# FFN block couples: weight sums made by accumulating DMAs on GpSimd's queue instead of VectorE additions

## The reference, cut to what matters

```python
f = jnp.square(jax.nn.relu(rmsnorm(x, g_pre_ffn) @ w1)) @ w2
x = x + rmsnorm(f, g_post_ffn)
```

## Time and profile before

| | us |
|---|---|
| median of 3 runs | 1749.37 |
| the runs | 1748.9, 1749.37, 1751.52 |
| profiled execution, first to last instruction (span) | 1748.0 |
| TensorE busy | 1736.1 (99%) |
| VectorE busy | 1208.1 (69%) |
| ScalarE busy | 798.3 (46%) |
| GpSimd busy | 16.3 (1%) |
| share of the 16 DMA engines, data moved | 25.4%, 149.06 MB |

### The profile page before, as it was taken

How to read it: one execution, slowest core, us unless ns; L and a number is a source line. 1 busy time by engine, 2 the same in 40 slices (tenths; PEclk the granted TensorE clock), 3 DMA queues, 4 the chain that set the end, 5 groups by cost and what they waited for, 6 DMA issues and landing times.

```text
span 1748.0 us, 31686 instructions
## 1 busy us (share of the span) xinstructions
PE 1736.1 (99%) x12975; PEld 1722.7 (99%) x12975; DVE 1208.1 (69%) x2376; ACT 798.3 (46%) x1589; POOL 16.3 (1%) x23
## 2 busy tenths in 40 slices
PE   9999999999999999999999999999999999999998
PEld 8999999999999999999999999999999999999997
DVE  7665555658698787668687555556677897777665
ACT  7634333335465454436366343334345545444452
POOL 0100000000000000000000000000000000000000
PEclk9999999999999999999999999999999999999998
DMA  4321212232213222322122222121313213222221
GB/s 176 114 82 61 91 61 82 72 95 82 85 48 98 86 97 89 94 97 97 63 106 77 82 72 82 62 91 60 103 63 108 80 44 120 87 91 79 84 97 55
DMA packets 52032, 149.06 MB, mean 85 GB/s; under 512 B 5552, under 2 KB 17072, under 8 KB 51888
## 3 DMA queue, kind: packets, MB, share of 16 engines
q1 hardware_dynamic: 50608, 144.94, 25.4%
q10 hardware_dynamic: 1280, 2.10, 0.4%
HBM read 143.15 MB, written 3.87 MB: 84 GB/s over the span
## 4 chain that ended last, share of the span: by engine, by line
PE 98%; DVE 1%; DMA 1%; ACT 0%; SPq 0%; issue 0%; DVEq 0%
PE ring L708 20%; PE ring L710 20%; PE ring L709 20%; PE att L708 11%; PE att L710 11%; PE att L709 11%; PE att L2976 1%; PE att L703 1%; PE att L702 1%; PE att L715 0%; DMA w_raw<-blocks_in 0%; PE att L716 0%; DMA x<-x_in 0%; PE att L2791 0%; PE att L3032 0%; DVE last L2745 0%
## 5 line engine op out<-in xcount | busy, mean ns | idle before, releaser
L708 PE MATMUL ring<-xs_hi,w_lo 128*128 128x288 f32 x2272 | 675.1, 297 | 1.5 <-DVE xs_lo L1756 1.2
L710 PE MATMUL ring<-xs_hi,w_hi 128*128 128x288 f32 x2272 | 669.3, 295 | 0.0
L709 PE MATMUL ring<-xs_lo,w_hi 128*128 128x288 f32 x2272 | 669.0, 294 | 0.0
L708 PEld LDWEIGHTS ring<-xs_hi,w_lo 128*128 128x128 f32 x2272 | 426.6, 188 | 4.4 <-DVE w_lo L1742 1.1
L709 PEld LDWEIGHTS ring<-xs_lo,w_hi 128*128 128x128 f32 x2272 | 426.8, 188 | 1.6
L710 PEld LDWEIGHTS ring<-xs_hi,w_hi 128*128 128x128 f32 x2272 | 426.5, 188 | 0.0
L1742 DVE TENSOR_TENSOR w_lo<-w_raw,w_hi 128x1024 fp32r<-128x1024 f32 (+1 forms) x334 | 332.6, 1019 | 58.2 <-ACT w_hi L1213 47.7
L710 PE MATMUL att<-f_hi,w_hi 128*128 128x288 f32 x960 | 283.2, 295 | 0.0
L709 PE MATMUL att<-f_lo,w_hi 128*128 128x288 f32 x960 | 282.9, 295 | 0.0
L708 PE MATMUL att<-f_hi,w_lo 128*128 128x288 f32 x960 | 282.6, 294 | 0.0
L708 PEld LDWEIGHTS att<-f_hi,w_lo 128*128 128x128 f32 x960 | 180.4, 188 | 0.0
(11 more groups left out here) (292 smaller groups left out, 2601.5 us busy)
## 6 DMA issues: line engine op xcount, KB each, us to landing
w_raw<-blocks_in SPq DMA_DIRECT2D x235, 512.0 KB, 3.6
small_raw<-small_in SPq DMA_DIRECT2D x16, 320.0 KB, 3.9
small_raw<-small_in SPq DMA_DIRECT2D x32, 128.0 KB, 3.9
x<-x_in SPq DMA_DIRECT2D x8, 288.0 KB, 6.9
small_raw<-small_in SPq DMA_DIRECT2D x8, 192.0 KB, 4.3
kv_out<-kv ACTq DMA_DIRECT2D x2, 576.0 KB, 4.4
x_out<-x SPq DMA_DIRECT2D x1, 1152.0 KB, 5.3
small_raw<-small_in SPq DMA_DIRECT2D x2, 512.0 KB, 5.1
```

The lines of the kernel that those rows point to most:

```text
L708: pe.matmul(out, w[1], x[0], start=first, stop=False)
L709: pe.matmul(out, w[0], x[1], start=False, stop=False)
L710: return pe.matmul(out, w[0], x[0], start=False, stop=last)
```

## The change: what it does

The four sums of a couple are no longer made by VectorE. SyncE loads base values into the slots of the sums, straight from the weights in HBM, and GpSimd's queue issues four DMAs that add to them:

- left slot (s[2]): SyncE loads a11 into both halves (one DMA whose source repeats, 512 KB); GpSimd adds a21 to both halves (512 KB, `left_first`), giving a11 + a21 twice; then it adds a22 to half 0 (256 KB, `sum2_made`). Half 0 is then S2, half 1 is S3.
- right slot (s[3]): SyncE loads a21 into half 0, GpSimd adds a22 (256 KB, `sum1_made`): S1. SyncE loads a12 into half 1, GpSimd adds half 0 of the left slot to it (256 KB, from SBUF, `sum4_made`): S4.

Each step waits for the semaphore of the one it builds on. Since the sums now only add, S1, S2, S3 are other sums than before (S2 = a11 + a21 + a22, S3 = a11 + a21), and four of VectorE's steps on the products subtract where they added; the count and size of these stays. a21 is no longer loaded to the slot of the second block, of which SyncE loads 256 KB. High parts are copied 1024 wide for each of the two slots (2 instead of 4), low parts subtracted in 4 instructions a couple instead of 6; `left_lo` waits for `sum4_made`, since it overwrites the raw S2 that the fourth addition reads. TensorE's matmuls are the same in number and size; their waits are on the new counts.

The core of the diff (GpSimd's part, SyncE's part, VectorE's order; the same is done to the other places that called the removed functions):

```diff
+        def weight_sums(L, g, p):
+            s, at = slots_pair(g, p), based(L, g, p)
+            a21, a22 = (blocks[L * NB + n_w1(g, 2 * p + 1)][:, 512 * k:512 * (k + 1)] for k in range(2))
+            left, sum2 = pl.slot(s[2])[2], pl.half_slot(s[2], 0)[2]
+            sum1, sum4 = (pl.half_slot(s[3], k)[2] for k in range(2))
+            pool.wait_ge(pl.left_based, at)
+            pool.dma_start(left.rearrange("p (b k) -> p b k", b=2), a21.unsqueeze(1).broadcast_to([P, 2, 512]),
+                           accum_op=ALU.add).then_inc(pl.left_first, 16)
+            pool.wait_ge(pl.sum1_based, at)
+            pool.dma_start(sum1, a22, accum_op=ALU.add).then_inc(pl.sum1_made, 16)
+            pool.wait_ge(pl.left_first, at)
+            pool.dma_start(sum2, a22, accum_op=ALU.add).then_inc(pl.sum2_made, 16)
+            pool.wait_ge(pl.sum2_made, at)
+            pool.wait_ge(pl.sum4_based, at)
+            pool.dma_start(sum4, sum2, accum_op=ALU.add).then_inc(pl.sum4_made, 16)
...
+            def next_couple(g, p, g1, p1):
+                after_pair(g, p, 1)
+                pair_load(g1, p1, 0)
+                after_pair(g, p, 3)
+                left_base(g1, p1)
+                after_pair(g, p, 4)
+                pair_load(g1, p1, 1)
+                after_pair(g, p, 5)
+                sum1_base(g1, p1)
+                after_pair(g, p, 6)
+                sum4_base(g1, p1)
...
             after_w2(0, 0)
             pair_load(2, 0, 0)
+            left_base(2, 0)
             after_w2(0, 1)
             pair_load(2, 0, 1)
+            sum1_base(2, 0)
+            sum4_base(2, 0)
+            next_couple(2, 0, 2, 1)
             pair_load(3, 0, 0)
             pair_load(3, 0, 1)
+            after_w2(0, 3)
+            left_base(3, 0)
+            sum1_base(3, 0)
+            sum4_base(3, 0)
...
+                after_w2(g - 1, 2)
+                    left_base(g + 1, 1)
+                after_w2(g - 1, 3)
+                    sum1_base(g + 1, 1)
+                    sum4_base(g + 1, 1)
...
             def outs_and_lo(g, k0, g0, p0, g1, p1):
-                pair_sums(g1, p1)
                 f_done(g0, p0, 2)
                 w2_out(g, k0)
                 f_done(g0, p0, 3)
                 w2_out(g, k0 + 1)
-                lo_a22(g1, p1)
-                lo_s3(g1, p1)
+                block_lo(g1, p1)
                 w2_out(g, k0 + 2)
-                lo_a11(g1, p1)
-                lo_s12(g1, p1)
-                w2_out(g, k0 + 3)
-                lo_a12(g1, p1)
-                lo_s4(g1, p1)
-                for k in range(k0 + 4, k0 + 8):
+                half_lo(g1, p1)
+                for k in range(k0 + 3, k0 + 8):
                     w2_out(g, k)
+                left_lo(g1, p1)
+                right_lo(g1, p1)
...
             w2_out(0, 9)
-            lo_s3(2, 0)
-            lo_a11(2, 0)
-            lo_s12(2, 0)
+            half_lo(2, 0)
+            left_lo(2, 0)
             w2_out(0, 10)
-            lo_a12(2, 0)
-            lo_s4(2, 0)
+            right_lo(2, 0)
             mix_lo(pl.ml[0][:, :, :], pl.mraw[0][:, :, :], pl.mh[0][:, :, :], 18, 2)
...
             pair_c12(2, 1)
+            left_lo(3, 0)
+            right_lo(3, 0)
...
             pair_c12(7, 0)
+            left_lo(7, 1)
+            right_lo(7, 1)
...
-                s1, s2, s3, s4 = (pl.half_slot(s[i], k) for i in range(2, 4) for k in range(2))
+                s2, s3, s1, s4 = (pl.half_slot(s[i], k) for i in range(2, 4) for k in range(2))
...
-                eng.wait_ge(pl.pair_lo, n + 3)
+                eng.wait_ge(pl.pair_lo, n + 1)
                 product(0, a11, x_at(0, 0))
-                eng.wait_ge(pl.pair_lo, n + 5)
                 product(1, a12, x_at(4, 0))
                 eng.wait_ge(pl.mix_lo, 8 * L + 3)
+                eng.wait_ge(pl.pair_lo, n + 3)
                 product(2, s2, mixed(1))
...
                 product(4, a22, mixed(3))
+                eng.wait_ge(pl.pair_lo, n + 4)
                 product(5, s1, mixed(0))
```

More of the change, by code:

```diff
@@ L743, in program @@
         loads(nc, block, pl, x_in, consts, tables, blocks, small, uv, cache_t, cache_n, cache_pe, x_out)
-        key_rotation(nc, block, pl)
+        rotation_and_sums(nc, block, pl, blocks)
         scalar_engine(nc, block, pl, x_in, x_out, kv_out, kpe_out, conv_out)
@@ L960, in _ @@
             key_rope(L, 1)
+            for g in range(FIRST_PAIR, GROUPS):
+                for p in range(2):
+                    weight_sums(L, g, p)
         for i, (m0, m1) in enumerate(TAIL_MOVED):
@@ L1522, in half_hi, with left_hi, right_hi @@
                 act.activation(hi, raw, ACT.Copy).then_inc(pl.pair_hi, 1)
-            def sum_hi(g, p, made, i, k):
-                hi, _, raw = pl.half_slot(slots_pair(g, p)[i], k)
-                eng.wait_ge(pl.pair_sum, 4 * pair_no(L, g, p) + made)
+            def left_hi(g, p):
+                hi, _, raw = pl.slot(slots_pair(g, p)[2])
+                eng.wait_ge(pl.sum2_made, based(L, g, p))
                 act.activation(hi, raw, ACT.Copy).then_inc(pl.pair_hi, 1)
[L1529 to L1533, removed]
+            def right_hi(g, p):
+                hi, _, raw = pl.slot(slots_pair(g, p)[3])
+                eng.wait_ge(pl.sum1_made, based(L, g, p))
+                eng.wait_ge(pl.sum4_made, based(L, g, p))
+                act.activation(hi, raw, ACT.Copy).then_inc(pl.pair_hi, 1)
             normed_hi(0, 0, 4)
@@ L1544, in _ @@
             half_hi(2, 0)
-            sums_hi(2, 0)
+            left_hi(2, 0)
+            right_hi(2, 0)
             first_copy(2, 0)
@@ L1552, in _ @@
             half_hi(2, 1)
-            sums_hi(2, 1)
+            left_hi(2, 1)
+            right_hi(2, 1)
             block_hi(3, 0)
             half_hi(3, 0)
-            sum_hi(3, 0, 1, 2, 0)
             first_copy(2, 1)
-            sum_hi(3, 0, 2, 3, 0)
-            sum_hi(3, 0, 3, 2, 1)
-            sum_hi(3, 0, 4, 3, 1)
             pair_c11(2, 1)
             pair_c21(2, 1)
+            left_hi(3, 0)
             pair_c22(2, 1)
             pair_c12(2, 1)
+            right_hi(3, 0)
             first_copy(3, 0)
@@ L1586, in _ @@
                 half_hi(g, 1)
-                sums_hi(g, 1)
                 if g < GROUPS - 2:
                     w2_hi(g, 0)
+                left_hi(g, 1)
+                right_hi(g, 1)
                 first_copy(g, 1)
@@ L1598, in _ @@
                 half_hi(g + 1, 0)
-                sums_hi(g + 1, 0)
+                if g < GROUPS - 2:
+                    w2_hi(g, 2)
+                left_hi(g + 1, 0)
+                right_hi(g + 1, 0)
             block_hi(7, 1)
             half_hi(7, 1)
-            sum_hi(7, 1, 1, 2, 0)
             first_copy(7, 0)
-            sum_hi(7, 1, 2, 3, 0)
-            sum_hi(7, 1, 3, 2, 1)
-            sum_hi(7, 1, 4, 3, 1)
             pair_c11(7, 0)
@@ L1609, in _ @@
             pair_c21(7, 0)
+            left_hi(7, 1)
             pair_c22(7, 0)
             pair_c12(7, 0)
+            right_hi(7, 1)
             first_copy(7, 1)
@@ L2440, in normed_lo @@
                 mix_lo(pl.xl[at], pl.xlraw[at], pl.xh[at], made, hi)
[L2442 to L2462, removed]
@@ L2478, in lo_s12, with pair_lo, block_lo @@
[L2478 to L2485, removed]
+            def pair_lo(g, p, views, hi):
+                eng.wait_ge(pl.pair_hi, 4 * pair_no(L, g, p) + hi)
+                minus(views[1], views[2], views[0]).then_inc(pl.pair_lo, 1)
+            def block_lo(g, p):
+                pair_lo(g, p, pl.slot(slots_pair(g, p)[0]), 1)
@@ L2487, in ring_of, with half_lo, left_lo, right_lo @@
+            def half_lo(g, p):
+                pair_lo(g, p, pl.half_slot(slots_pair(g, p)[1], 1), 2)
+            def left_lo(g, p):
+                eng.wait_ge(pl.sum4_made, based(L, g, p))
+                pair_lo(g, p, pl.slot(slots_pair(g, p)[2]), 3)
+            def right_lo(g, p):
+                pair_lo(g, p, pl.slot(slots_pair(g, p)[3]), 4)
             def ring_of(g, p, i):
```

111 lines of the change are left out of this document (54 added, 57 removed).

## The result

The changed kernel takes 1849.7 us (median of 4 runs, 1844.26 to 1857.62) against 1749.36 us: ratio 1.0575, 95% interval 1.0548 to 1.0603. It is 100 us slower. The forecast was 1763.4 us, slower by 14 us, with a range that ended at 1825 us; the measured time lies above it. It falls into rival (b), a wait in every couple, and beyond what that rival's own arithmetic gives for the chain that was measured, about 1795 us at X = 16.8 (X is the sum of the three accumulates from issue to landing, as in the prediction). The profiled execution took 1844.26 us, with a span of 1842.4 us.

The account below looks back on a forecast made before the run. TensorE was taken to bound the kernel, with VectorE's relief worth 0 us. Waits of 7.0 us a layer, 14.0 us in all, on 1748.0 gave 1762.0, plus 1.4 for the median: 1763.4 us; range 1748.5 to 1825 us.

Parts of the forecast that it names:

- rival (b): Before product 2: accumulates take over 15.8 us, every couple waits; 1824 us at 18, 1909 us at 21.6; chance 0.28.
- What bounds the kernel: TensorE, busy 99% of the span, never waits in the FFN; VectorE's 66 us removed are worth 0 us.
- rival (c): VectorE's freed 66 us give TensorE something, at most the 4.2 us of all waits, 1745 us; chance 0.03.
- (d): High and low parts stay, work doesn't move; ends as with nearly plain-priced accumulates, 1749.4 us; chance 0.28 shared with that case.
- Base of the left slot: SyncE's 512 KB load before the accumulates, after product 3 of the couple before (4, 0): lands in 3.6 us.
- The price of an accumulate: GpSimd's three dependent additions into the left slot: 5.6, 4.2 and 4.2 us, 14.0 us in sum.
- second read: Accumulate also reads its destination: 1.4 us more for 512 KB, 0.7 us for 256 KB.
- The room: Nine couples a layer behind w2 work: 1.8 us to spare before product 2, 0 us cost; chain decides from 15.8 us.
- The one-off couples: Waits at (3, 0), (7, 1) and (2, 0): 4.9 + 1.4 + 0.7 = 7.0 us a layer, 14.0 us in all.
- The rule on GpSimd's descriptors: GpSimd can't write DMA descriptors during VectorE's two-port modes; `tensor_tensor` has none, so a wait in every couple is less likely.

## Why the prediction was wrong

- **What bounds the kernel: right.** VectorE's relief was worth nothing (1749.42 us with its additions and all the rest of the change); rival (c) is out, and so is (d).
- **Base of the left slot: mis-sized.** I took a quiet 512 KB load, 3.6 us; before (4, 0) the first addition started 4.5 us after the base was issued, and before (3, 0), in the kernel without the fourth addition, 4.7 us.
- **The price of an accumulate: mis-sized, all three links the same way.** 5.6 / 4.2 / 4.2 us predicted, 7.0 / 5.0 / 4.8 measured, X = 16.8 instead of 14.0. My parts were a second read of 1.4 and 0.7 us and 0.6 us for GpSimd. The kernel with copies separates the parts. Without the addition the three links take 11.3 us, and 3.6 + 2.9 + 2.9 with 0.6 us each for GpSimd is 11.2: that part was right in sum, by luck: the long link was 1.4 us dearer than 4.2, the one inside SBUF 1.2 us cheaper than 3.5. The additions themselves are 1.4 + 1.6 + 2.5 = 5.5 us where I had 1.4 + 0.7 + 0.7 = 2.8: right for the long link, two to three and a half times too little for the short ones, the one inside SBUF above all. The step that failed is the term for the second read, scaled from how plain transfers grow with size.
- **The room: right, and this was the step that decided.** Together the chain was 0.9 + 2.8 = 3.7 us longer than forecast, against 1.8 us to spare, so 1.9 us should be missing in each of the 18 couples that I had at 0 us, 34 us in all. Measured are 55.4 us: 2.8 us on average in the 16 from (3, 1) to (7, 0), and 5.4 and 5.5 us at the two (2, 1), where the first link took 9 us. The medians leave out that spread, whose cause is open. I had put the edge at X = 15.8 and gave what lies past it 0.28; it should have had more, since every unmeasured part of the price could only add.
- **The one-off couples: right in place, wrong beside the others.** (3, 0) waits 7.6 us where nothing before it does (without the fourth addition), though 4.9 was predicted for a chain with one link more. In the changed kernel it waits 1.8 us only, because (2, 1) just before it waits 5.4 us and gives its chain that time. Such waits don't add: the six one-off couples have 8.8 us of waits together and not 14.0. At (7, 1) the forecast also lacked a step, the order of GpSimd's queue (from SyncE and GpSimd):

```profile
834.83 0.38 SPq L885 DMA_DIRECT2D w_raw<-blocks_in  x1
...
841.10 0.87 POOL L1004 DMA_DIRECT2D w_raw<-w_raw  x1 [5.12 <-DMA w_raw<-blocks_in]
841.64 1.56 POOL L996 DMA_DIRECT2D w_raw<-blocks_in  x1
```

Its first addition starts 6.8 us after its base was issued, right behind the last addition of (7, 0).

- **What a wait costs: missing, and this step failed too.** Every case, rival (b) too, priced a wait at its length. At X = 18 it gave 1824 us; the real kernel, with 64 us of waits, took 1849.7, 31 us of it in matmuls at the lower clock. The waits put in by hand show that this term belongs to the wait and not to the DMAs.
- **The rule on GpSimd's descriptors** (the Trainium skill, "SBUF — State Buffer", "Who interferes with whom") was not tested; GpSimd's time for one kind of DMA hardly varies (859 to 925 ns for S1's and nearly all of S2's) beside a VectorE busy for half the time, mostly with `tensor_tensor`, which fits it.

## What to carry to other kernels

Price a chain of dependent DMAs by its number of links, at 5 us for each accumulate of 256 KB and 7 us for 512 KB here, with single ones up to 9 us, and hold it against the room on the engine that must not stop; the busy share of that engine's neighbours says nothing about it. Where TensorE is at its limit, waits of 2 to 4 us were paid about one and a half times over on average (94 us of span for 64 us of waits), since behind some of them the matmuls ran at half speed for up to 6 us, so the margin has to be several microseconds. Work taken from an engine that nobody waits for gains nothing, and this can be read beforehand from an empty list of waits.

## What the runs showed of the hardware that I had not expected

- TensorE's granted clock fell behind 14 of the 22 waits of the changed kernel and behind 15 of the 24 of nearly equal length put in by hand, and behind none of 1.1 us: 64.5 us of waits in 25 places, 2.6 us each, cost 30 us more busy time, mean clock 0.982; 27.1 us in 25 places, 1.1 us each, cost 5.6 us, mean clock 0.997. After one wait of 3.75 us the clock stood at 0.50 for about 6 us. Waits of the same 2.67 us were followed by 0.50 in one place and by 1.00 in another.
- An accumulating DMA takes 1.8 times the packets of a copy of the same bytes (16896 against 9216). The dearest addition, against its copy, is the one from SBUF into SBUF: 4.8 against 2.3 us for 256 KB.
- A plain copy of 256 KB on GpSimd's queue lands in 3.4 us (S2's line), no later than one of SyncE's in the same kernel (3.5 us). For 512 KB whose source repeats it is 5.6 us, against 4.2 us for SyncE's load of that kind, the left base.
